# Hybrid encoder step: the split weights in one array, blocks of odd k moved by 128 bytes, and 32 extra products at the end

## The reference

```python
a_x, a_g, bq, bk, bv, cq, ck, cv, cf = split(x @ w_in)        # 2048 -> 5124
y = concat(rms(rglru(a_x) * gelu(a_g)), rms(band(bq, bk, bv)), rms(fox(cq, ck, cv, cf)))
x = layer_norm(ALPHA * x + y @ w_out)                          # 2048 -> 2048
hdn = square(relu(x @ w_up))                                   # 2048 -> 8192
return layer_norm(ALPHA * x + hdn @ w_down)                    # 8192 -> 2048
```

## Time and profile before

| | |
|---|---|
| Median of three runs | 2238.35 us |
| Profiled execution | 2238.34 us, of which the span of its instructions is 2236.6 us |
| TensorE busy with products | 2217.5 us, 99% of the span |
| VectorE, ScalarE, GpSimd busy | 77%, 46%, 10% |
| Clock granted to TensorE | 1.00 in all 40 slices of the page |

### The profile page before, as it was taken

The page is one execution under the profiler, slowest core; times in us unless marked ns, Lnnn a source line. Parts: engine busy times, 40 slices in busy tenths (PEclk is TensorE's granted clock), DMA queues, the critical chain, the costliest instruction groups (busy, mean ns, idle before and its releaser), DMA issues.

```text
span 2236.6 us, 38368 instructions
## 1 busy us (share of the span) xinstructions
PE 2217.5 (99%) x16391; PEld 2176.6 (97%) x16391; DVE 1711.4 (77%) x1305; ACT 1029.6 (46%) x990; POOL 217.8 (10%) x269
## 2 busy tenths in 40 slices
PE   9999999999999999999999999999999999999998
PEld 8999999998889999999999999999999999999997
DVE  5757999974566765777778777778778778878887
ACT  4534656644453555644434444364335335335243
POOL 2000211200202022000000000001001001001002
PEclk9999999999999999999999999999999999999999
DMA  8665565574424476565444544577778678659765
GB/s 295 228 217 163 183 219 164 187 271 157 139 93 153 178 269 235 180 230 193 146 173 168 187 154 164 193 268 215 210 231 245 169 234 252 193 162 298 240 213 181
DMA packets 119493, 450.12 MB, mean 201 GB/s; under 512 B 14032, under 2 KB 38264, under 8 KB 80832
## 3 DMA queue, kind: packets, MB, share of 16 engines
q1 hardware_dynamic: 76128, 357.69, 44.2%
q0 software_dynamic: 16432, 47.92, 11.6%
q10 hardware_dynamic: 26800, 42.58, 5.2%
HBM read 371.12 MB, written 78.59 MB: 201 GB/s over the span
## 4 chain that ended last, share of the span: by engine, by line
PE 90%; DVE 5%; ACT 2%; DMA 2%; issue 1%; ACTq 0%; DVEq 0%
PE psum L3025 57%; PE psum L2758 19%; PE psum L2995 5%; PE psum L516 4%; DMA raw<-in_w_down 1%; PE psum L2970 1%; DVE w_lo L2102 1%; PE psum L2836 1%; PE psum L2920 1%; PE psum L2936 1%; DVE x_e_lo L2242 1%; PE psum L3187 0%; PE psum L2787 0%; ACT w_hi L1465 0%; DVE y_rows L2492 0%
## 5 line engine op out<-in xcount | busy, mean ns | idle before, releaser
L3025 PE MATMUL psum<-x_e_hi,w_hi 128*128 128x288 f32 x1600 | 474.5, 297 | 1.2 <-DVE w_lo L2102 1.1
L3025 PE MATMUL psum<-x_e_hi,w_lo 128*128 128x288 f32 x1600 | 474.2, 296 | 0.0
L3025 PE MATMUL psum<-x_e_lo,w_hi 128*128 128x288 f32 x1600 | 466.7, 292 | 0.0
L3025 PE MATMUL psum<-x_b_hi,w_hi 128*128 128x288 f32 x1536 | 455.2, 296 | 1.3 <-DVE w_lo L2108 0.8
L3025 PE MATMUL psum<-x_b_hi,w_lo 128*128 128x288 f32 x1536 | 455.3, 296 | 0.0
L3025 PE MATMUL psum<-x_b_lo,w_hi 128*128 128x288 f32 x1536 | 447.9, 292 | 0.0
L3025 PEld LDWEIGHTS psum<-x_e_lo,w_hi 128*128 128x128 f32 x1600 | 304.8, 190 | 0.0
L3025 PEld LDWEIGHTS psum<-x_e_hi,w_hi 128*128 128x128 f32 x1600 | 300.7, 188 | 3.0 <-DVE w_lo L2102 2.8
L3025 PEld LDWEIGHTS psum<-x_e_hi,w_lo 128*128 128x128 f32 x1600 | 300.0, 187 | 0.0
L3025 PEld LDWEIGHTS psum<-x_b_lo,w_hi 128*128 128x128 f32 x1536 | 292.8, 191 | 0.1
L3025 PEld LDWEIGHTS psum<-x_b_hi,w_hi 128*128 128x128 f32 x1536 | 288.6, 188 | 2.2 <-issue 1.9
(11 more groups left out here) (424 smaller groups left out, 4739.6 us busy)
## 6 DMA issues: line engine op xcount, KB each, us to landing
raw<-in_w_down SPq DMA_DIRECT2D x61, 1024.0 KB, 6.9
raw<-in_w_up SPq DMA_DIRECT2D x54, 1024.0 KB, 5.6
raw<-in_w_in SPq DMA_DIRECT2D x31, 1024.0 KB, 6.4
a_even<-in_w_down SPq DMA_DIRECT2D x30, 1024.0 KB, 7.3
raw<-in_w_out SPq DMA_DIRECT2D x24, 1024.0 KB, 4.8
a_even<-in_w_up SPq DMA_DIRECT2D x24, 1024.0 KB, 5.8
h_scratch<-c_tile ACTq DMA_DIRECT2D x48, 288.0 KB, 2.1
down_scratch<-c_tile POOLq DMA_DIRECT2D x45, 288.0 KB, 5.3
```

Source lines behind the costliest of these rows:

```text
L3025: mm = pe.matmul(PS[:, bank, 0:HALF], w, x[:, k, :], start=(k + n == 0), stop=(k == UK - 1 and n == 2))
```

## The change

The four arrays of split weights become views of one array, `w_split`, of two parts. The first part holds the blocks of even k of `w_hi0`, `w_hi1`, `w_lo0` and `w_lo1`, the second the blocks of odd k. Behind the first part 32 columns (128 bytes) stay unused, so all blocks of odd k start 128 bytes further on, at a multiple of 256. A filler further behind is smaller by the 256 bytes that the array has grown, so that the tiles of activations keep their addresses. Behind the last product TensorE waits for `rows_c` to reach 20 and then makes 32 products of 288 columns into bank 0 of PSUM, which nobody reads. Their stationary operands start at a multiple of 256, and their moving ones at 224, 96, 0 and 128 past one, eight of each.

```diff
-        WH = [sb(f"w_hi{s}", [128, UK, UC], F32R) for s in range(2)]
-        WL = [sb(f"w_lo{s}", [128, UK, UC], F32R) for s in range(2)]
+        WS = sb("w_split", [128, 2, 2 * UK * UC + 32], F32R)
+        WH, WL = ([WS[:, :, UK // 2 * UC * (2 * i + s):UK // 2 * UC * (2 * i + s + 1)].rearrange("p q (j c) -> p q j c", c=UC) for s in range(2)] for i in range(2))
...
-        sb("behind_last", [64, 128])
+        sb("behind_last", [64, 64])
...
+        def by_pairs(T):
+            return T[:, :, :].rearrange("p (j q) c -> p q j c", q=2)
...
-                act.activation(WH[u % 2][:, :, :], src[:, :, :], ACT.Copy).then_inc(hi_done, 1)
+                act.activation(WH[u % 2], by_pairs(src), ACT.Copy).then_inc(hi_done, 1)
...
-                dve.tensor_tensor(WL[par][:, :, :], src[:, :, :], WH[par][:, :, :].bitcast(F32), ALU.subtract).then_inc(lo_done, 1)
+                dve.tensor_tensor(WL[par], by_pairs(src), WH[par].bitcast(F32), ALU.subtract).then_inc(lo_done, 1)
...
-                    a, b = WH[s][:, k, 128 * m:128 * m + 128], WL[s][:, k, 128 * m:128 * m + 128]
+                    a, b = WH[s][:, k % 2, k // 2, 128 * m:128 * m + 128], WL[s][:, k % 2, k // 2, 128 * m:128 * m + 128]
...
+            pe.wait_ge(rows_c, 20)
+            for x_at, w_at in ((0, 32), (32, 32), (8, 32), (40, 32)):
+                for n in range(8):
+                    x, k = flat(F2[n // 4]), n % 4
+                    w = WS[:, 0, :]
+                    pe.matmul(PS[:, 0, 0:HALF], w[:, UC * (n % 7) + w_at:UC * (n % 7) + w_at + 128], x[:, TOK * k + x_at:TOK * k + x_at + HALF], start=True, stop=True)
```

More of the change, by code:

```diff
@@ L456, in hi @@
             act.wait_ge(unit_done, G * 2 + (s + 1))
-            act.activation(WH[s][:, :, :], RAW[s][:, :, :], ACT.Copy).then_inc(hi_done, 1)
+            act.activation(WH[s], by_pairs(RAW[s]), ACT.Copy).then_inc(hi_done, 1)
         def pair_k(p):
@@ L495, in hi_piece @@
             k = pair_k(p)
-            act.activation(WH[a % 2][:, k, :], RAW[a % 2][:, k, :], ACT.Copy).then_inc(hi_done if p == 3 else piece_hi, 1)
+            act.activation(WH[a % 2][:, :, p, :], RAW[a % 2][:, k, :], ACT.Copy).then_inc(hi_done if p == 3 else piece_hi, 1)
         def lo_piece(dve, a, p):
@@ L501, in lo_piece @@
             k = pair_k(p)
-            dve.tensor_tensor(WL[a % 2][:, k, :], RAW[a % 2][:, k, :], WH[a % 2][:, k, :].bitcast(F32), ALU.subtract).then_inc(lo_done if p == 3 else piece_lo, 1)
+            dve.tensor_tensor(WL[a % 2][:, :, p, :], RAW[a % 2][:, k, :], WH[a % 2][:, :, p, :].bitcast(F32), ALU.subtract).then_inc(lo_done if p == 3 else piece_lo, 1)
         def lo(dve, G, s):
             dve.wait_ge(hi_done, G * 2 + (s + 2))
-            dve.tensor_tensor(WL[s][:, :, :], RAW[s][:, :, :], WH[s][:, :, :].bitcast(F32),
+            dve.tensor_tensor(WL[s], by_pairs(RAW[s]), WH[s].bitcast(F32),
                               ALU.subtract).then_inc(lo_done, 1)
+        def by_pairs(T):
+            return T[:, :, :].rearrange("p (j q) c -> p q j c", q=2)
         def products(pe, m, s, k, kk, X, Y, first, final, to=None):
             to = m if to is None else to
-            a, b = WH[s][:, k, 128 * m:128 * m + 128], WL[s][:, k, 128 * m:128 * m + 128]
+            a, b = WH[s][:, k % 2, k // 2, 128 * m:128 * m + 128], WL[s][:, k % 2, k // 2, 128 * m:128 * m + 128]
             last_mm = None
@@ L1445, in _ @@
             act.wait_ge(unit_done, N_1B + 1)
-            act.activation(WH[0][:, :, :], SIG2[:, :, :], ACT.Copy).then_inc(hi_done, 1)
+            act.activation(WH[0], by_pairs(SIG2), ACT.Copy).then_inc(hi_done, 1)
             finish_c00(N_SB // 2 - 1, 0)
@@ L1452, in hi_1b @@
                 act.wait_ge(unit_done, n + 1)
-                act.activation(WH[par][:, :, :], src[:, :, :], ACT.Copy).then_inc(hi_done, 1)
+                act.activation(WH[par], by_pairs(src), ACT.Copy).then_inc(hi_done, 1)
             def squared(T, scale):
@@ L1464, in hi_a @@
                 act.wait_ge(unit_done, phase_a(su) + a + 1)
-                act.activation(WH[a % 2][:, :, :], buf[:, :, :], ACT.Copy).then_inc(hi_done, 1)
+                act.activation(WH[a % 2], by_pairs(buf), ACT.Copy).then_inc(hi_done, 1)
             def f2_hi(su):
```

18 lines of the change are left out of this document (9 added, 9 removed).

## The result

The changed kernel takes 2227.06 us (median of 5, 2224.19 to 2228.43); before takes 2238.35 us (median of 5, 2237.26 to 2238.43). The ratio is 0.9949, 95% interval 0.9938 to 0.9959: 11.3 us or 0.5% faster.

The account below looks back on a forecast made before the run. The prediction took TensorE's product pace and the last microseconds as the bound. Its terms, −0.5 plain products, −1.6 F4, −0.1 first units, −0.2 line 2995, summed to −2.4 us on 2238.34: 2236.0 us, range 2229 to 2248.

Parts of the forecast that it names:

- What bounds the kernel: TensorE busy 2217.5 of 2236.6 us: only the products' pace and the last microseconds can move the time.
- Plain products: 12,048 products, mainly line 3025: two thirds meet a next block at 96, one third at 224; 132.20 against 132.24 ns, −0.5 us.
- The bounds: Plain products: −7.1 us if all reach the pace of distance 96, +12.9 us if all come to that of 224.
- F4 and line 2995: 1824 products of `x_e` without hi or lo: 132.48 against 133.33 ns, −1.6 us; line 2995's units: +0.2 and −0.4 us.
- The first units: First five units, 240 products: five of six meet distance 96, 131.93 against 132.49 ns, −0.1 us.
- Splitting passes: ScalarE and VectorE passes over eight runs of 256 cost 0; VectorE's 22% slack covers a faster TensorE.
- The extra products: 32 products behind the last one, 4.3 us, hidden beside SyncE's last store with 1.6 us to spare.
- The tail: End of the kernel: nothing added; a slow start of the extra products would bring +1.1 us.
- The sum: −0.5 − 1.6 − 0.1 − 0.2 = −2.4 us on 2238.34 us, forecast 2236.0 us.
- The own distance: Rival, chance 0.25: a product's pace goes by its own two operands, plain products all at 96; 2230.8 us.
- A third at 224 spoiling the rest: Rival, chance 0.20: runs of two at 96 are too short, plain products come to 133.31 ns; +12.9 us, 2251 us.
- only the moving tile's address counts: Rival, chance 0.15: 224 may be a moving tile's good start and 96 the bad; nothing changes, 2238.3 us.

Follow-up runs that it names:

- all at 0: Kernel before with its split weights 128 bytes further on, so every stationary block starts at 0 modulo 256: 2237.73 us, ratio 0.9998.
- the map: Changed kernel with 16 groups of 48 products in place of its 32, both starts fixed in each group; read by pace, 131.7 to 133.4 ns.
- all at 224: Changed kernel without extra products, whole weight array 128 bytes further on, so each plain product's own distance is 224: 2246.29 us, ratio 1.0029.
- the patterns run: Changed kernel with 16 groups of 48 products in place of its 32, varying the order in which starts alternate; read by pace, 131.11 to 134.44 ns.
- group 9: 48 products behind the changed kernel's last one, both starts moving after every six, own distance 96: 131.67 ns.

## Why the prediction was wrong

*What bounds the kernel.* Right: the products' pace moved the time, and the waits and the clock of the tail took a part of that back (below). That the paces differ by distance was right too, and is now shown with the stationary operand moved (all at 0) and in the map.

*Plain products: the step that failed.* "Two of three products in a k meet a block of the same k (distance 96). The third meets one of the next k. That is 224" gave 132.20 ns; it is 131.10. The step took the load that runs beside a product for the one that sets its pace. The load does run there, but for the plain products the pace follows each product's own pair: 131.1 ns with all at 96, 132.2 with half and half, mostly 133.3 with all at 224. An order in which every next block is at 96 gave 132.2. The term was −0.5 us and is (131.10 − 132.24) × 12,048 = −13.7. The own distance is not a full rule either: F4 runs at 133.33 ns with a third of its products at 96 and at 132.7 with a half.

*The bounds.* The lower end, −7.1 us, took 131.65 as the fastest pace, the pace of a constant pair at 96. Alternating pairs in runs of three reach 131.11, below every fp32r row of before, and 12,048 × 0.55 = 6.6 us lie between that end and the truth. This alone carried the time out of the range. No row had both operands moving, so none said that 131.65 was a floor, and the only lower one, 121.25 ns, was set aside as too far. That it is the pace of one of two passes is a reading which no run here tests.

*F4 and line 2995.* Forecast 132.48 and 132.24; measured 132.71 for F4, 132.27 and 132.24 for the two stretches of line 2995: −1.1 us in place of −1.6 for F4, −0.2 as said for line 2995. The first units, forecast at 131.93 (−0.1 us), ran at 27.52 / 209 = 131.67 in the window that answers to 28.22 / 213. For F4 and line 2995 the wrong rule gives about the right value, since by either rule good and bad meetings mix; that was luck, and that such checks agree did not show the rule. The first units don't mix by their own distance, they are all at 96, and 131.67 is what runs of six at 96 gave in the patterns run (group 9); their term is (131.67 − 132.49) × 240 = −0.2 us.

*Splitting passes.* Their own time was right: 2292 against 2293 ns, 1921 against 1920. That VectorE's slack of 22% covers a faster TensorE was taken from the mean over the main part. TensorE's waits for `w_lo` of line 2102 (now 2105) went from 1.1 to 2.7 us, and this had no term. In the nine profiled executions of kernels with plain products at 131.1 ns these waits come to 1.2 to 4.6 us, in the five at 132.2 ns or more to 0.2 to 1.6. That fits a TensorE which gets ahead of VectorE at single units; the ranges overlap, and no run tests it alone.

*The extra products.* Right: hidden, with no measurable cost (0.9941 without them, 0.9949 with them, intervals overlapping).

*The tail.* "The prediction is wrong if the pace of line 3025 leaves 131.9 to 132.5 ns, or if more than 1 us is added in the tail." Both came: 1.8 us were added in the profiled execution, by the clock behind the 2.1 us gap and not by the extra products, which this step had suspected. The idle time stood in the trace of before, with the clock at 1.00, and got no term. In the changed kernel's second profiled execution, where the clock held, the tail is only 0.2 us longer than before.

*The sum.* The products' terms come to −13.7 − 1.1 − 0.2 − 0.2 = −15.2 us, up to the transposes 13.1 are measured, and the tail gives 1.8 back: −11.3. Of the 2.1 us between 15.2 and 13.1, 0.4 come from taking one window for the whole: over the whole trace the mean time from start to start (gaps over 160 ns left out) fell by 1.10 ns at line 3028, 1.07 at line 2761 and 0.5 in F4, and by 0.35 at line 519, which was forecast at 0; with line 2998 that is 14.8 us. Most of the rest are the waits for `w_split` above, 2.7 − 1.1 = 1.6 us. They differ from execution to execution: in the second one of the changed kernel only 2219.47 − 2210.05 = 9.4 us were gained up to the transposes.

*The rivals.* The own distance was the right mechanism, with the time 3.7 us too high at 2230.8: its pace was 0.55 ns too slow, and it gave nothing to F4. A third at 224 spoiling the rest did not happen, and that only the moving tile's address counts is refuted by all at 0. The Trainium skill's rule in TensorE: Matmul & The Clock Gate (Step-by-step: what each phase is for), that a weight load takes no read bandwidth from the running product, would have made the shift worth nothing. The runs differ by 2.2 ns in each product, 131.1 against 133.3, by the distance alone. They do not show whether that is bandwidth or something else.

**Open.** No rule on pairs, own or next, gives all of the groups: the run's length counts in no simple order, distance 0 is good when constant and poor when alternating, F4 doesn't follow the share of its products at 96, and one pair, one pattern in one kernel (all at 224) and one program in two executions (the first units) have two paces. It looks as if something holds a phase from product to product; what it is was not found.

## What to carry to other kernels

Where TensorE is the bound and small products follow each other, look at where both operands start modulo 256 bytes: pushing half of the stationary blocks 128 bytes on was worth 1.1 ns in each product here, and the wrong half costs as much. Measure the pattern in the kernel's own order: the map of constant pairs had the sign right and the size wrong for distances 96 and 224, and for distance 0 it promised a gain where the kernel got slower. A faster pace also moves the waits for other engines, so read them one by one and not from the mean slack. When several layouts of before fit a rule, ask which of them only mix its cases, and don't take the fastest row seen for a floor when the change makes a pattern that no row has.

## What the runs showed of the hardware

- The pace of a 288-column fp32r product at 2.4 GHz goes from 131.1 to 134.4 ns with the operands' starts and their order alone (130.5 for the first units in one execution). Most paces are whole multiples of four cycles in three products: 131.11, 131.67, 132.22, 132.78 and 133.33 ns are 944, 948, 952, 956 and 960.
- Of the distances between moving and stationary start modulo 256, in steps of 32, constant pairs ran at 131.7 at 0 and 96, at 132.2 to 132.3 at 64 and at 133.3 to 133.4 at the others. No dependence on either address alone or on the address modulo 512 was seen.
- The same pair of starts modulo 256 ran at 131.67 ns, or at 133.33 for 144 products on end, by what had run before it. In the kernel with all at 224, 204 units of plain products ran at 133.3 ns and 30 at 132.8.
- Behind 1.9 to 3.0 us without a product the granted clock was at half for 3.4 us in four profiled executions (0.51 over a window of 3.5 us in the changed kernel), and it stayed at 1.00 behind 2.0 to 2.6 us in eight others, one of them of the changed kernel too.
